# Three reorderings in the attention stage of a two-block transformer: adds before their reader, gains before a softmax step, the Fourier copy after one, and a wait raised from 5 to 6

## The reference, cut to what matters

```python
def diff_attend(q, k, v, lam):
    s = jnp.einsum('bqhmd,bkhmd->bhmqk', q, k).astype(jnp.float32)
    p = jax.nn.softmax(s, axis=-1)
    a = p[:, :, 0] - lam * p[:, :, 1]
    return jnp.einsum('bhqk,bkhe->bqhe', a.astype(v.dtype), v)
...
def fourier_mix(f):
    ...
    y = jnp.fft.fft2(fg, axes=(1, 3), norm='ortho').real
...
def ada_params(cond, w_ada, b_ada):
    m = jax.nn.silu(cond) @ w_ada + b_ada
    return jnp.split(m[..., None, :], 6, axis=-1)
```

## Time and profile before

| | |
|---|---|
| median of 3 runs | 1920.31 us (1919.19 to 1923.19) |
| the profiled execution | 1920.31 us, span 1918.4 us |
| busy share of the span | PE 76%, DVE 26%, ACT 12%, POOL 4% |
| share of DMA engines' span taken by the loads' queue | 91.5% |
| chain that ended last | DMA 54%, PE 34%, DVE 6%, issue 2%, POOL 2% |
| attention stage of layer 0 | about 680 to 852 us of the span |

### The profile page before, as it was taken

How to read it: one execution, slowest core, us unless ns; L and a number is a source line. 1 busy time by engine, 2 the same in 40 slices (tenths; PEclk the granted TensorE clock), 3 DMA queues, 4 the chain that set the end, 5 groups by cost and what they waited for, 6 DMA issues and landing times.

```text
span 1918.4 us, 28873 instructions
## 1 busy us (share of the span) xinstructions
PE 1451.2 (76%) x12714; PEld 797.8 (42%) x12714; DVE 489.7 (26%) x970; ACT 239.2 (12%) x584; POOL 83.0 (4%) x92
## 2 busy tenths in 40 slices
PE   9888996767688899998766656556999766556655
PEld 5445542333333354655423323224866422323322
DVE  4774421111112049942000000004543100000001
ACT  3122220111211122321000000001001000000000
POOL 2210000000000023200000000000000000000000
PEclk9998999898898999999778778888999887988777
DMA  9544999999999987579999999999987999999997
GB/s 362 198 185 161 365 400 423 420 421 420 417 418 415 413 326 292 211 320 370 421 421 418 423 419 423 420 418 386 363 346 306 418 422 421 418 423 419 422 420 296
DMA packets 123090, 717.73 MB, mean 374 GB/s; under 512 B 5969, under 2 KB 10833, under 8 KB 98385
## 3 DMA queue, kind: packets, MB, share of 16 engines
q1 hardware_dynamic: 121536, 713.11, 91.5%
q10 hardware_dynamic: 1424, 2.71, 0.4%
HBM read 714.75 MB, written 1.05 MB: 373 GB/s over the span
## 4 chain that ended last, share of the span: by engine, by line
DMA 54%; PE 34%; DVE 6%; issue 2%; POOL 2%; ACT 1%; SPq 1%; ACTq 0%; DVEq 0%
DMA ring<-in_moe_w_up 35%; DMA ring<-in_w_down 11%; PE bank L1622 5%; PE bank L2537 4%; PE bank L505 4%; DMA ring<-in_w_gate 4%; DMA ring<-in_moe_w_down 4%; PE bank L1613 3%; PE bank L1670 3%; PE bank L946 2%; PE bank L977 1%; PE bank L649 1%; PE bank L2295 1%; PE bank L339 1%; PE bank L1696 1%
## 5 line engine op out<-in xcount | busy, mean ns | idle before, releaser
L1622 PE MATMUL bank<-ring,arena 128*32 128x256 f32 x3968 | 298.9, 456 | 160.0 <-DMA ring<-in_moe_w_up 98.9
L1670 PE MATMUL bank<-ring,arena 128*32 128x256 f32 x2912 | 240.5, 486 | 176.5 <-DMA ring<-in_moe_w_down 136.9
L1622 PEld LDWEIGHTS bank<-ring,arena 128*32 128x32 f32 x3968 | 145.3, 127 | 292.9 <-issue 107.8
L1670 PEld LDWEIGHTS bank<-ring,arena 128*32 128x32 f32 x2912 | 116.0, 134 | 290.2 <-issue 174.9
L1613 PE MATMUL bank<-ring,arena 128*32 128x512 f32 x976 | 131.2, 651 | 58.7 <-DMA ring<-in_w_up 29.4
L505 PE MATMUL bank<-ring,low 128*128 128x512 f32 (+1 forms) x352 | 151.9, 582 | 1.6 <-DMA ring<-in_w_in 1.1
L1742 DVE TENSOR_TENSOR arena<-arena,bank 128x128 f32<-128x128 f32 (+1 forms) x64 | 22.7, 355 | 507.3 <-PE bank L1622 503.9
L1696 PE MATMUL bank<-arena 32*128 32x256 f32 x1024 | 94.6, 440 | 16.9 <-PE bank L1696 10.6
L505 PEld LDWEIGHTS bank<-ring,low 128*128 128x128 f32 x352 | 65.9, 194 | 69.2 <-issue 68.1
L1748 ACT ACTIVATE arena<-bank 128x256 f32<-128x256 f32 x64 | 24.6, 384 | 555.3 <-PE bank L1683 552.2
L1757 DVE TENSOR_TENSOR arena<-bank,gate_strips 128x256 f32<-128x256 f32 x32 | 13.6, 425 | 300.1 <-PE bank L1670 300.1
(11 more groups left out here) (315 smaller groups left out, 1363.2 us busy)
## 6 DMA issues: line engine op xcount, KB each, us to landing
ring<-in_moe_w_up SPq DMA_DIRECT2D x64, 2048.0 KB, 26.7
ring<-in_moe_w_gate SPq DMA_DIRECT2D x60, 2048.0 KB, 25.5
ring<-in_moe_w_down SPq DMA_DIRECT2D x60, 2048.0 KB, 27.0
ring<-in_w_up SPq DMA_DIRECT2D x31, 2048.0 KB, 26.2
ring<-in_w_down SPq DMA_DIRECT2D x31, 2048.0 KB, 26.1
ring<-in_w_gate SPq DMA_DIRECT2D x30, 2048.0 KB, 25.1
ring<-in_ada_w SPq DMA_DIRECT2D x24, 2048.0 KB, 13.2
ring<-in_attn_w_in SPq DMA_DIRECT2D x8, 2048.0 KB, 20.8
```

The source lines that it names most:

```text
L1622: last = nc.tensor.matmul(GU[up][32 * j:32 * j + 32, 0:QW], xgT[:, x + kk, a:a + C], w[:, kq, j * QW:(j + 1) * QW], start=(kk == 0), stop= ...
L1670: last = nc.tensor.matmul(z_bank(M)[32 * j:32 * j + 32, 0:QW], act_s[:, b, q * C:(q + 1) * C], w[:, kq, j * QW:(j + 1) * QW], start=(kk == ...
```

## The change

Four edits, three of them of the order in `steps2`: in units 8 to 11 the two conditioning adds come before `ada_use` where they came behind it; in the same units the single add and `gain u` come before the second `attend2` where they came behind it; `fourier_first` comes behind `attend2(9)` where it came ahead of it; and PE starts `fourier_proj 0` once `vput` is 6 (both copies of units 12 and 13 are out) where 5 was enough (that of unit 12).

```diff
@@ fourier_proj_pe
             if b == 0:
-                nc.tensor.wait_ge(h2["vput"], 5)
+                nc.tensor.wait_ge(h2["vput"], 6)
@@ steps2
                 if u != 10:
                     yield "ada_sum", (u + 3) // 2
+                yield "ada_add", 2
                 if u != 10:
                     yield "ada_use", (u + 3) // 2
-                yield "ada_add", 2
                 yield "proj", (u, (1,))
                 yield "tr", u - 1
                 yield "sum", u
+                yield "ada_add", 1
+                yield "gain", u
                 if u > 8:
                     yield from attend2(s + 1)
-                yield "ada_add", 1
-                yield "gain", u
                 yield "ada_add", 2 if u == 8 else 1
...
             yield "fourier_proj", 1
-            yield "fourier_first", 0
             yield from attend2(9)
             yield "ada_add", 3
+            yield "fourier_first", 0
             yield "fourier_chan", 0
```

## The result

The changed kernel takes 1934.03 us (median, 1932.54 to 1935.5) against 1921.32 us before (1919.19 to 1923.19) in four runs each: 12.7 us, ratio 1.0066 with a 95% interval of 1.0049 to 1.0084. It is slower, as forecast, but by more than the 8.0 us of the sum, and outside the range, whose upper end was 1932.0.

What follows compares the result with a forecast made beforehand. PE's arrival at the experts' weights was taken to shift the load stream one to one, with DVE and PE near full before it. PE's 4.7 us plus 3.3 for two clock falls gave 8.0: 1928.3 us, range 1920.3 to 1932.0.

Steps and rivals of the forecast that it cites:

- the sum: Total forecast loss: PE 4.7 us late at scores 10 plus 3.3 for two falls of the clock, 8.0 us.
- Part 1 in unit 8: Adds ahead of ada_use: transposes of unit 7 2.5 us later, PE's gap 3.2, PE left about 1.0 late.
- Part 1 in unit 11: Adds ahead of ada_use: transposes of unit 10 come behind two adds, 2.0 us, delaying a chain of three engines.
- Part 3: Wait for vput 6: new PE gap of 2.5 us ahead of L2079, DVE 1.95 late at maximum 8.
- Part 4: fourier_first behind attend2(9): PE gap of 3.2 us ahead of L2089, scores 10 at 814.3, PE 4.7 late.
- part 2: Gain ahead of second softmax step: gaps of 1.7 and 1.6 us ahead of scores 4 and 6, maximum 7 0.7 late.
- the likeliest case: One or two falls of the clock behind the new PE gaps, chance 0.46; with two falls, 1928.3 us.
- Faster: Rival: PE's 2.55 gap ahead of unit 11's transposes and its slow stretch go, 4.2 us, 1916.1; chance 0.09.
- no change: Rival: the stream of loads decides and hides what PE loses, 1920.3 us; chance 0.14.
- slower with one fall at most: Rival: no fall of the clock behind any but one gap, 1925.0 to 1926.7 us; chance of none 0.13.
- The case of the gaps' length: Rival: the clock falls behind all three new long PE gaps, 1930.0 us; chance of three or more falls 0.18.
- the 5 to 9 that I named: Sign in the profile after: scores 10 some 5 to 9 us later than at 808.94.

Runs made afterwards that it cites:

- adds_only: Only the two adds moved ahead of ada_use in units 8 to 11, on the kernel before: ratio 1.0031 (1.0020 to 1.0043), stretch +6.2 us.
- adds_unit11: The two adds moved ahead of ada_use in unit 11 only, on the kernel before: ratio 1.0014 (1.0005 to 1.0023), stretch +2.0 us.
- wait_only: Only PE's wait for vput 6 ahead of fourier_proj 0, on the kernel before: ratio 1.0003 (0.9990 to 1.0015), stretch +1.1 us.
- adds_gain: Both order edits of units 8 to 11, neither Fourier edit, on the kernel before: ratio 1.0042 (1.0029 to 1.0055), stretch +8.0 us.
- all_four_warm: The changed kernel plus idle matmuls in PE's four long gaps: ratio 1.0046 (1.0033 to 1.0059) against the kernel before, stretch +8.5 us.
- gain_warm: Kernel before with only the gain edit, plus idle matmuls ahead of scores 4 and 6: ratio 1.0010 (1.0000 to 1.0021), stretch +1.4 us.
- gain_no_add: Kernel before with gain ahead of the second softmax step, but both adds behind that step: ratio 1.0010 (0.9998 to 1.0022), stretch +1.1 us.
- wait_copy: Both Fourier edits (vput 6, fourier_first moved), no order edits of units 8 to 11, on the kernel before: ratio 1.0034 (1.0021 to 1.0047), stretch +6.5 us.
- gain_then_adds: Kernel before with only gain and the single add behind the second softmax step exchanged: ratio 0.9999 (0.9991 to 1.0008), stretch -0.4 us.

## Why the prediction was wrong

**What held.** That PE's lateness at the end of the stage is paid in full (12.1 us between the two traces, both at scores 11 and at the chain's first wait for experts' weights, 902.35). Part 1 in unit 8: 1.0 and a fall of the clock of 1.65 make 2.65; maximum 2 was 2.55 late (757.61, against 756.84 in the timeline before). That is in part luck: in adds_only the same gap made maximum 2 late by 4.2. Part 1 in unit 11: 2.0 forecast, 2.0 in adds_unit11. Part 3: 1.25 from maximum 7 to maximum 8; in the trace after 1.3, in wait_only 1.1 for the whole; PE's gap was 1.54 and not 2.5, and the clock stayed up behind it. Part 4: from maximum 9 on 2.75 and a fall of the clock make 4.4; after, maximum 9 is 9.3 late and scores 11 13.9, that is 4.5.

**What failed is part 2.** It carried DVE from 1.0 late (2.65 with the fall of unit 8) to 0.7 (2.35) at maximum 7. The trace after has 8.0 there (798.91 against 792.68, and 1.8), and adds_gain has the same without the Fourier edits. The missing 5.7 us come from two things, both at one place in the sum:

- *"I expect no fall of the clock behind it."* I credited part 2 with the present slow stretch ahead of unit 11's transposes (1.65), and gave none to the gaps that it makes ahead of scores 4 and 6, the late exponentials. These gaps were 2.27 and 2.51, not 1.7 and 1.6, and the clock fell behind both. Against all_four_warm that cost 1.5 and 2.9, together 4.4, where the sum had nothing. gain_warm shows the same by experiment: the gain edit costs 1.4 instead of 5.4 with the gaps filled. A bound for one such fall stood in the text (1931.6), but I left them out of the likeliest case.
- *"Behind sum (0.8) and one add (1.2), DVE waits 2.6 - 2.0 = 0.6 for the root."* The root's price came from a row at which no add ran beside it. With the add beside it the root takes 1.0 more, and DVE waits 1.53 instead of 0.6, twice: 1.9. The root is behind DVE's sum and ahead of the gain, which is ahead of the exponential that PE waits for, so it lengthened PE's gaps too. gain_no_add shows it.

4.4 + 1.9 = 6.3, and PE reaches scores 7 in the trace after 6.4 later than the forecast had it (797.75 and 1.8, against 791.5 and the 1.65 of unit 8). The forecast had DVE come to maximum 7 some 0.7 later than scores 7 allowed (793.4, against 791.5 + 1.16), and that room absorbs as much: 5.7. The two score maps behind a late exponential come 0.66 us apart, as in the 1.79 of the earlier trace rows, which I counted at scores 10 and not at scores 6; but it fills the forecast gap of 0.3 and little is left of it (7.09 in all_four_warm from scores 6 to scores 7, against 6.95 forecast). 8.0 and 5.7, with 0.2 that parts 3 and 4 came out longer, are the 13.9 of the stretch, within the 9.4 to 16.1 us of the time's interval. This working is read from single executions.

The rule of the Trainium skill on the clock ("TensorE: Matmul & The Clock Gate", section "HAM oscillation") did no better alone: the falls did not sort by the length of the gap. The clock fell behind 2.02 (all_four_warm), 2.27 and 2.51 (the change), 2.32 (wait_copy) and 2.33 (gain_then_adds), and stayed up behind 2.18 (adds_unit11), 2.39 and 2.54 (wait_copy).

The slowness of the root is a rule that I had at hand and did not use. The Trainium skill, "SBUF — State Buffer", section "SBUF: two separate sides", says of the ports that VectorE and GpSimd share that whoever takes them first keeps them for the whole instruction while the other stands still, and that this holds for VectorE operations with two SBUF inputs beside a GpSimd operation that reads SBUF. The traces agree: one add of 1.28 lengthens POOL's work by 1.0 (2.60 against 1.63, 3.17 against 2.19), two by 2.0 (4.15), and the maximum, which reads PSUM, by nothing. The roots of the first units of the same stage have an add beside them; the one at 708.89 us in the trace before takes 2.60, and that row would have given the price.

```profile
708.71 1.28 DVE L409 SCALAR_TENSOR_TENSOR arena<-ring,condT,arena 128x1024 f32<-128x1024 f32 x1
```

```profile
708.89 2.60 POOL L277 TENSOR_TENSOR small<-small,columns 128x8 f32<-128x8 f32 x1 [15.43 <-DVE small L267]
```

**The rivals.** "Faster" and "no change" are out. So is slower with one fall at most. The case of the gaps' length had three falls and 1930.0; there were four: two of them where it had none (scores 4 and 6), and none behind the gap of part 3, where it had one. Scores 10 came 14.4 late, outside the 5 to 9 that I named.

Not settled: which gaps of 2.0 to 2.6 us end at 1.2 GHz. The same gap ahead of unit 11's transposes did in the execution before and did not in wait_copy: 5.65 against 4.02 us from these transposes to scores 7. How long the slow stretch lasts varies as well: behind the gap of 3.3 in unit 8 it cost 1.5 us in the changed kernel and 3.0 in adds_only. So one place can differ by 1.5 us or so between executions.

## What to carry to other kernels

Price an operation from a row that has the same neighbours: the same root took 1.6 or 2.6 us, depending on whether a VectorE add with two SBUF inputs ran beside it. If two engines are both nearly full, moving work "over" a wait helps only if nobody is queued behind what is pushed back; here the pushed-back exponentials opened gaps on TensorE, and the work at half clock behind such gaps was 5.4 of the 13.9 us. Filler work (here the conditioning adds) belongs where its own engine idles, behind the busy stretch; the one version built so was the only one that beat the kernel before, by 2.9 us.

## What the runs showed of the hardware that I had not expected

A POOL operation with SBUF operands takes about 1.0 us longer for each VectorE add of 1.28 us with two SBUF inputs beside it: the rotation takes 2.19, 3.17 and 4.15 us with none, one and two adds beside it. And idle matmuls of 128 columns from a broadcast column, filling gaps of 2.3 to 3.3 us, kept the clock at 2.4 GHz (all_four_warm: 1.00 behind all four). But PE then came earlier to a later wait, whose gap grew from 1.54 to 2.02, and the clock fell there. A fall has no fixed price: 1.5 us and 3.0 us behind the same gap of 3.3 in two runs.
